# Two gate tiles per mLSTM head instead of three, thirds of a half tile, rows and gate in memory of their own

## The reference, cut to what matters

```
u = rmsnorm(x) * (1 + scale) + shift
aq, ak, av, az, mq, mk, mv, mo, mz, mg, ga, gb = split(u @ w_in)
y_b = attention(aq, ak, av) * silu(az)                      # 16 heads of 64
per mLSTM head of 256 (4 heads):
    h = forward scan + backward scan of (mq, mk, mv, gates) from the state C, n
    y_a = head_norm(h) * sigmoid(mo) * silu(mz)
merged = sigmoid(ga) * (y_a @ w_proj_a) + sigmoid(gb) * (y_b @ w_proj_b)
out = x + gate * rmsnorm(merged @ w_out)
```

## Time and profile before

| | us |
|---|---|
| median of 3 runs | 1960.53 (1960.12 to 1960.54) |
| profiled execution, its own time | 1960.23 |
| its span in the trace | 1958.4 |
| PE busy in the span | 1925.1 |
| DVE busy | 1204.3 |
| ACT busy | 667.2 |
| POOL busy | 109.8 |

### The profile page before, as it was taken

How to read it: one execution, slowest core, us unless ns; L and a number is a source line. 1 busy time by engine, 2 the same in 40 slices (tenths; PEclk the granted TensorE clock), 3 DMA queues, 4 the chain that set the end, 5 groups by cost and what they waited for, 6 DMA issues and landing times.

```text
span 1958.4 us, 31714 instructions
## 1 busy us (share of the span) xinstructions
PE 1925.1 (98%) x12298; PEld 1785.3 (91%) x12298; DVE 1204.3 (61%) x2065; ACT 667.2 (34%) x1015; POOL 109.8 (6%) x195
## 2 busy tenths in 40 slices
PE   6999999999999999999999999999999999999998
PEld 2589999999999999999898999889889999988886
DVE  3268766666666666665666664565556767783224
ACT  3443333333333333332555554233224222242221
POOL 2010000000000000000000000000002000000000
PEclk9999999999999999999999999999999999999999
DMA  9952353333333333334632323364454666634224
GB/s 372 398 181 77 114 166 112 112 112 112 112 112 112 112 112 112 112 112 114 196 98 82 123 83 118 91 150 134 109 130 143 196 208 184 209 114 140 81 75 161
DMA packets 297838, 273.95 MB, mean 140 GB/s; under 512 B 20016, under 2 KB 245048, under 8 KB 295840
## 3 DMA queue, kind: packets, MB, share of 16 engines
q1 hardware_dynamic: 283632, 216.71, 37.6%
q0 software_dynamic: 13824, 55.92, 7.9%
q10 hardware_dynamic: 304, 0.25, 0.0%
HBM read 235.01 MB, written 40.44 MB: 141 GB/s over the span
## 4 chain that ended last, share of the span: by engine, by line
PE 91%; DMA 3%; DVE 3%; SPq 1%; issue 1%; ACT 1%; POOL 0%; DVEq 0%; POOLq 0%; ACTq 0%
PE bank L2030 20%; PE bank L2110 12%; PE bank L2103 12%; PE bank L2104 12%; PE bank L2326 11%; PE bank L2039 10%; DMA WORK<-in_w_ada_dram 2%; PE bank L1949 2%; PE bank L2230 2%; PE bank L2005 2%; PE bank L2219 1%; PE bank L2171 1%; PE bank L2232 1%; PE bank L2148 1%; PE bank L1985 1%
## 5 line engine op out<-in xcount | busy, mean ns | idle before, releaser
L2030 PE MATMUL bank<-XH,WH 128*128 128x320 f32 x1472 | 345.5, 316 | 2.8 <-DVE XL L1823 2.1
L1026 ACT ACTIVATE WH<-RAW 128x1024 fp32r<-128x1024 f32 x195 | 206.6, 1060 | 386.3 <-PE bank L2110 306.3
L2030 PE MATMUL bank<-XL,WH 128*128 128x320 f32 x1472 | 335.2, 309 | 0.0
L1458 DVE TENSOR_TENSOR WL<-RAW,WH 128x1024 fp32r<-128x1024 f32 x195 | 238.4, 1222 | 142.3 <-ACT WH L1026 142.3
L905 ACT ACTIVATE WH<-RAW 128x1024 fp32r<-128x1024 f32 x122 | 129.1, 1059 | 530.5 <-PE bank L2039 406.1
L2030 PEld LDWEIGHTS bank<-XH,WH 128*128 128x128 f32 x1472 | 244.5, 188 | 10.8 <-issue 8.0
L2030 PEld LDWEIGHTS bank<-XL,WH 128*128 128x128 f32 x1472 | 246.2, 188 | 0.0
L2039 PE MATMUL bank<-XH,WL 128*128 128x320 f32 x1472 | 235.9, 310 | 0.0
L2039 PEld LDWEIGHTS bank<-XH,WL 128*128 128x128 f32 x1472 | 220.1, 188 | 4.1 <-issue 3.8
L2104 PE MATMUL bank<-XL,WH 128*128 128x320 f32 x720 | 212.5, 309 | 0.0
L2103 PE MATMUL bank<-XH,WH 128*128 128x320 f32 x720 | 212.4, 309 | 0.0
(11 more groups left out here) (241 smaller groups left out, 2968.8 us busy)
## 6 DMA issues: line engine op xcount, KB each, us to landing
RAW<-in_w_in_dram SPq DMA_DIRECT2D x165, 512.0 KB, 3.8
WORK<-in_w_ada_dram SPq DMA_DIRECT2D x71, 512.0 KB, 8.9
proj_dram<-OUTS POOLq DMA_DIRECT2D x92, 320.0 KB, 2.5
RAW<-in_w_out_dram SPq DMA_DIRECT2D x32, 512.0 KB, 3.7
RAW<-in_w_ada_dram SPq DMA_DIRECT2D x25, 512.0 KB, 9.2
WORK<-proj_dram SPq DMA_DIRECT2D x16, 640.0 KB, 4.6
WORK<-proj_dram POOLq DMA_DIRECT2D x32, 320.0 KB, 3.3
RAW<-in_w_proj_a_dram SPq DMA_DIRECT2D x16, 512.0 KB, 4.7
```

The costliest lines, as they stand in the source:

```text
L1026: ins = nc.scalar.activation(WH[:, (j + p) % 2, :], pair_raw(j, p), ACT.Copy)
L1458: V.tensor_tensor(WL[:, w, :], pair_raw(j, p), WH[:, w, :].bitcast(F32), ALU.subtract)\
L2030: pe.matmul(banks[n][:, 0:HALF_TOK], wh[:, k, :], x[:, k0 + k, n * HALF_TOK:(n + 1) * HALF_TOK], start=(first and k == 0 and wi == 0), sto ...
```

## The change

- `T_L1` goes from 64 to 68, `T_L2` from 78 to 82, `L2_TILES` from 3 to 2. Four gate tiles move from the plain tiles beside the mLSTM to two more pairs.
- A step goes with a third of a half tile: 16 products instead of 24. r = 1 to 12 now lie over two tiles.
- `HH` and the output gate (`MG`) get memory of their own. The row loads wait for `ml_qs` instead of `ml_ht`, the keys for `ml_sp` instead of `ml_zg`; the queries still wait for `ml_zg`. `states_out`, `state_loads` and the values of the next head follow each other.
- PE's backward state goes from r = 10 to 11, its transposes and DVE's gating from r = 11 to 12. On DVE the gate products stay at r = 10, the copy of the backward state (`ml_cbd`) goes to r = 11, in front of `lo`.
- The merge takes `w_proj_b` on the attention's blocks first. ACT makes their high parts before `ml_ya`, DVE five of their low parts at the last head's r = 11.
- POOL's power follows the gate loads in the same step, and a buffer for POOL's own DMA descriptors is set to 4096.

```diff
-T_PAIR, T_L1, T_L2, T_MERGE, T_OUT, T_END = 4, 64, 78, 90, 106, 122
+T_PAIR, T_L1, T_L2, T_MERGE, T_OUT, T_END = 4, 68, 82, 90, 106, 122
-L1_TILES, L2_TILES = 14, 3
+L1_TILES, L2_TILES = 14, 2
+LOW_EARLY = 5
+        HH = sb("HH", [P, 5, MD])
+        MG = sb("MG", [P, 2, TOK])
...
@@ SP
-                    sp.wait_ge(ml_zg, h)
+                    sp.wait_ge(ml_sp, h)
                 head_rows(h, MK, RB_MK, ml_kv)
...
-                    sp.wait_ge(ml_ht, h)
+                    sp.wait_ge(ml_qs, h)
                 for r in range(2):
                     sp.dma_start(RB[:, r, :], ...)
...
-                    if s == (3 if h == 0 else 6 * h + 3):
+                    if s == 4 * h + 3:
                         if h == 0:
                             head_values(0)
-                        head_keys(h)
-                        if h:
+                            head_keys(0)
+                        else:
+                            row_loads(h)
+                            head_keys(h)
                             head_queries(h)
-                    if s == 6 * h + 4:
+                    if s == 4 * h + 4:
                         if h == 0:
                             head_queries(0)
                             row_loads(0)
-                        if h:
+                        else:
                             states_out(h - 1)
-                    if s == 6 * h + 5:
-                        state_loads(h)
-                        if h + 1 < M_HEADS:
-                            head_values(h + 1)
+                            state_loads(h)
+                            if h + 1 < M_HEADS:
+                                head_values(h + 1)
@@ POOL
                     pool.wait_ge(ml_ub, 4 * h + 4)
-                    pool.wait_ge(ml_kw, h + 1)
-                    pool.dma_start(MK, head_rows(RB_MO, h)).then_inc(ml_gates_in, 16)
+                    pool.dma_start(MG[:, :, :], head_rows(RB_MO, h)).then_inc(ml_gates_in, 16)
                     pool.dma_start(MVT, head_rows(RB_MZ, h)).then_inc(ml_gates_in, 16)
-                if k == 2:
                     pool.wait_ge(ml_var, h + 1)
@@ ACT
-            act.wait_ge(ml_ya, M_HEADS + 1)
+            act.wait_ge(yb_done, 10 * KV_HEADS + 1)
             act.wait_ge(w_used, 2 * T_MERGE - 1)
-            high_y(range(8), y_hi)
+            high_y(range(8), y_hi, 8)
             evac(0, T_MERGE - 1)
             hi(0, 0, 2 * T_MERGE + 1)
+            act.wait_ge(ml_ya, M_HEADS + 1)
@@ DVE
+                    if r == 11:
+                        dve.wait_ge(ml_cb, h + 1)
+                        for cc in range(2):
+                            ins = V.tensor_copy(CA[:, 1, cc, :], ab[2 + cc][:, 0:257])
+                        ins.then_inc(ml_cbd, 1)
-                    if r == 11:
+                    if r == 12:
                         dve.wait_ge(ml_ht, h + 1)
...
-                if part and s + 1 < 2 * L2_TILES * M_HEADS:
+                if part == 1 and s + 1 < 2 * L2_TILES * M_HEADS:
                     lo(0, 0, 2 * T_L2 + s + 1)
+                if q == 6 * L2_TILES * M_HEADS - 2:
+                    low_y(range(LOW_EARLY), y_hi, y_lo, 8)
                 for h, r in phases(q):
                     if r == 10:
-                        dve.wait_ge(ml_cb, h + 1)
-                        for cc in range(2):
-                            ins = V.tensor_copy(CA[:, 1, cc, :], ab[2 + cc][:, 0:257])
-                        ins.then_inc(ml_cbd, 1)
                         z = MVT.rearrange("p c t -> p (c t)")
                         dve.wait_ge(ml_eg, h + 1)
...
+            low_y(range(LOW_EARLY, 8), y_hi, y_lo, 8)
             lo(0, 0, 2 * T_MERGE)
-            low_y(range(3, 8), y_hi, y_lo)
+            low_y(range(8, 12), y_hi, y_lo, 8)
             lo(0, 0, 2 * T_MERGE + 1)
-            low_y(range(8, KT), y_hi, y_lo)
+            low_y(range(12, KT), y_hi, y_lo, 8)
@@ PE
-                if r == 11:
+                if r == 12:
                     pe.wait_ge(ml_h, h + 1)
...
-                    if r == 10:
+                    if r == 11:
                         pe.wait_ge(ml_upd, h + 1)
                         state(1).then_inc(ml_cb, 1)
                 if part == 0:
...
-                    high_products(banks, w, 8 * x, range(0, 4), x == 0)
-                else:
-                    high_products(banks, w, 8 * x, range(6, 8), x == 0)
+                    high_products(banks, w, 8 * x, range(0, 3), x == 0)
+                elif part == 1:
+                    high_products(banks, w, 8 * x, range(4, 7), x == 0)
+                else:
                     pe.wait_ge(lo_done, 2 * t + x + 1)
-                    low_products(banks, w, 8 * x, x == 1, range(0, 4))
+                    low_products(banks, w, 8 * x, x == 1, range(0, 6))
                 for h, r in phases(q):
                     inside(h, r)
                 if part == 0:
-                    high_products(banks, w, 8 * x, range(4, 6), x == 0)
-                else:
-                    low_products(banks, w, 8 * x, x == 1, range(4, 8)).then_inc(w_used, 1)
-            pe.wait_ge(ml_ya, M_HEADS + 1)
+                    high_products(banks, w, 8 * x, range(3, 4), x == 0)
+                elif part == 1:
+                    high_products(banks, w, 8 * x, range(7, 8), x == 0)
+                else:
+                    low_products(banks, w, 8 * x, x == 1, range(6, 8)).then_inc(w_used, 1)
```

More of the change, by code:

```diff
@@ L674, in row_loads, with merge_half @@
                 if h:
-                    sp.wait_ge(ml_ht, h)
+                    sp.wait_ge(ml_qs, h)
                 for r in range(2):
                     sp.dma_start(RB[:, r, :], rrow[h + 4 * r, :].partition_broadcast(P)).then_inc(ml_in, 16)
[L679 to L682, removed]
+            def merge_half(i, k, x):
+                g = 2 * (T_MERGE + k) + x
+                w_half(4 * i + (g - 3), g, g % 4, (w_pb_v, w_pa_v)[x][:, :, bass.ds(P * k + 2 * P * i, P)])
+            for s in range(2 * L2_TILES * M_HEADS + 4):
+                if s < 2 * L2_TILES * M_HEADS:
+                    in_tile(T_L2 + s // 2, 0, COL_MERGE + P * (GATES_PAIRED + L1_TILES + s // 2), (s % 2,))
+                else:
+                    merge_half(0, (s - 16) // 2, s % 2)
                 for h in range(M_HEADS):
-                    if s == (3 if h == 0 else 6 * h + 3):
+                    if s == 4 * h + 3:
                         if h == 0:
                             head_values(0)
-                        head_keys(h)
-                        if h:
+                            head_keys(0)
+                        else:
+                            row_loads(h)
+                            head_keys(h)
                             head_queries(h)
-                    if s == 6 * h + 4:
+                    if s == 4 * h + 4:
                         if h == 0:
@@ L693, in _ @@
                             row_loads(0)
-                        if h:
+                        else:
                             states_out(h - 1)
-                    if s == 6 * h + 5:
-                        state_loads(h)
-                        if h + 1 < M_HEADS:
-                            head_values(h + 1)
+                            state_loads(h)
+                            if h + 1 < M_HEADS:
+                                head_values(h + 1)
+                    if s == 5 and h == 0:
+                        state_loads(0)
+                        head_values(1)
             def gada_load(i, m):
@@ L715, in out_piece @@
                 w_half(8 * n + (g - 3), g, g % 4, w_out_v[:, 2 * q:2 * q + 2, bass.ds(512 * n, 512)], k=2)
-            for k in range(2):
-                for x in range(2):
-                    merge_half(0, k, x)
             states_out(M_HEADS - 1)
@@ L862, in merge_gates @@
             def merge_gates(j, u):
-                for gi, rb in ((0, RB_GA), (1, RB_GB)):
+                for gi, rb in ((0, RB_GB), (1, RB_GA)):
                     pool.dma_start(GAB[:, u, gi, :], proj[bass.ds((rb + j) * P, P), :]).then_inc(sig_in[u], 16)
@@ L1161, in inter @@
                 nc.scalar.activation(ENM[:, :, :], COLH[:, :, 2:4], ACT.Exp).then_inc(ml_w, 1)
-            for q in range(4 * L2_TILES * M_HEADS):
-                s, part = divmod(q, 2)
+            for q in range(6 * L2_TILES * M_HEADS):
+                s, part = divmod(q, 3)
                 if part == 0:
@@ L1681, in _, with low_y @@
                         low_keys(kv, 3)
+            def low_y(ks, high, done, shift=0):
+                for k in ks:
+                    dve.wait_ge(high, k + 1)
+                    V.tensor_tensor(XL[:, k, :], Y[:, (k + shift) % KT, :], XH[:, k, :].bitcast(F32),
+                                    ALU.subtract).then_inc(done, 1)
             dve.wait_ge(m0_in, 16)
```

21 lines of the change are left out of this document (6 added, 15 removed).

## The result

The changed kernel takes 1975.67 us (median of 6 runs, 1972.78 to 1977.97); the kernel before took 1960.47 us beside it (1959.26 to 1960.66). The ratio is 1.0077, 95% interval 1.0067 to 1.0087: slower by 15.2 us. The forecast was 1967.4 us, range 1956 to 1974: the direction was right, the size was half of what came, and the median lies outside the range. The profiled execution took 1972.78 us, with a span of 1970.6 (before 1958.4, so +12.2).

A forecast was written before the change was run, and what follows sets the result against it. TensorE, never waiting in the mLSTM, was taken to bound the kernel. Terms -7.04 (products), +12.4 (hand-over), +1.2 (head 0) and +0.3 (merge's entry) sum to +6.9 us: forecast 1967.4 us, range 1956 to 1974.

The forecast's parts named there:

- 48 products, -7.04: Two pairs replace four plain tiles beside the mLSTM; PE saves 48 products, 7.04 us.
- The hand-over of `ab[2]`: r = 8 to 12 of each head: PE waits 3.1 us for DVE's copy of the backward state, +12.4 in all.
- Rival 1: The hand-over of `ab[2]` costs next to nothing, DVE's overhang being absorbed: 1955.0 us; chance 0.15.
- rival 3: The stall at the hand-over is halved: 1961.2 us, no change that shows; chance 0.09.
- Row of the head before, queries, scaled queries, gates hidden: mLSTM heads: `ml_ya`, next queries, read-out's scaled queries and gate loads come in time; no added wait of PE.
- Head 0, 1.2: First mLSTM head: rows and queries still wait for the attention, so PE waits for the transposed copies, +1.2 us.
- Merge's entry, +0.3: Start of the merge: PE waits for DVE's low parts, 3.7 us lost against 3.4 before, +0.3.
- State loads, taken as 0: Read-outs: loads behind the previous head's stores; one reading gave a 3.3 us stall in three heads, zero was taken.
- Rival 2: State loads come late, read-outs wait up to 3.3 us in heads 1 to 3: 1977.3 us; chance 0.10.
- The smaller buffer, taken as hidden: POOL's descriptor buffer at 4096 costs no instruction, and even DMAs that wait for one another would be hidden.
- The clock, taken as unaffected: TensorE's granted clock stays at 1.00 despite the new pauses in the mLSTM; nothing added.
- rival 4: Clock falls to 1.2 GHz after each 3.1 us pause, 4 x 3.7 = 15 us more: 1982; chance 0.02.

The follow-up runs named there:

- e9: e8 with nothing on DVE beside POOL's power, one `lo` in DVE's idle time, gate products behind the copy, forward state stored ahead of the queries: 1954.67 us.
- e1: The changed kernel with both gate products on DVE made over 8 of 1280 columns: 1960.32 us.
- e3: The kernel before, with only the copy of the backward state moved behind the gate products on DVE: 1975.99 us.
- e4: The kernel before with POOL's descriptor buffer at 4096 and nothing else: 1961.56 us.
- e2: The changed kernel with 20 overwritten filler products on PE between the fourth and fifth transpose of each head: 1970.81 us.
- e8: e7, with PE taking high by high, low weights, then low parts of `Y` for the merge's first tile: 1966.42 us.
- e5: The changed kernel with a head's state stores issued ahead of the step's weight half on SP: 1973.14 us.
- e10: e9 with the norm weight's load issued on ACT's queue instead of POOL's: 1955.40 us.
- e6: The changed kernel with DVE reordered: first gate product during POOL's power, normalising, backward copy, second product, `lo` behind the gating: 1967.39 us.
- e7: e6 with state stores first, a semaphore of their own for queries, and head 0's transposed copies ahead of its decay arguments: 1968.27 us.

## Why the prediction went wrong

By its own steps:

- **48 products, -7.04:** right. 32 pairs at 24.68 us. The span of e9, which waits almost nowhere, is 1951.2, 7.2 under before: -7.0 for the products, -1.0 for shorter waits at the merge's entry, +0.8 for the four small waits elsewhere.
- **The hand-over of `ab[2]`, 3.1 us per head:** right, 2.97 measured. That DVE's order makes it was shown from both sides: e1 without the two products' time, e3 with the order alone on the kernel before. Rival 1 (absorbed) and rival 3 (halved) are out.
- **Row of the head before, queries, scaled queries, gates hidden:** right; no wait of PE at any of them in heads 1 to 3.
- **Head 0, 1.2:** 1.40 measured.
- **Merge's entry, +0.3:** about right in price, though after doesn't show it: of the 2 us that I named before the sixth block 0.31 came, since the low clock ahead of it had slowed PE. Without that, in e1, the two waits are 1.71 and 0.29, together 2.0 as before (2.05).
- **State loads, taken as 0:** mis-sized. Rival 2's mechanism was there, 1.26 and 0.57 us. First store to first load took 15.8 us in head 1 and not the 9 that I read off the last head; the row with the store between two heads was the nearer one. The bound of 3.3 held in every experiment (2.87 at most).
- **The smaller buffer, taken as hidden:** a miss of 1.36 us in the profile of after, 0.87 of PE's time in the trace of e4. I looked at POOL in the mLSTM only; the DMA that it delays stands 230 us later, and behind it DVE.
- **The clock, taken as unaffected: the step that failed.** The sum with what was measured in all other terms is 1967.4 - 0.5 (waits 11.86, not 12.4) + 0.2 + 1.8 + 1.4 - 0.4 (merge, -0.1 for +0.3) = 1969.9, inside the range. In the profiled execution the clock adds 1.8 net, and with the 1.1 that isn't listed that is its 1972.8, still inside. The median is 2.9 higher. e2, which takes only the four pauses' low clock away, gains 4.9 us of median (about 1 to 7 by the intervals). By that the clock is the largest of the three terms that I had put at nothing; that it makes up all of the 2.9 us is not shown. I gave rival 4 a chance of 0.02 on one row: a stretch at the start of the program whose 4.6 us of idle time came in many pieces, beside work of another kind. A pause of 3 us in the mLSTM is not that, and the row was one draw: in the traces of e1, e2 and e8 the clock does fall for 3.4 to 6.8 us in this opening, between 22 and 30 us. The Trainium skill, TensorE: Matmul & The Clock Gate, Part 1: The HAM clock gate, was the better guide to the direction; the traces agree in part: of after's four pauses of 2.95 to 2.97 us two were followed by a low stretch, of e3's four all. My price in the rival was too high in the other way, 3.7 us for each pause instead of 1.2 to 1.6 for each low stretch.

What stays open: which pauses are followed by a low stretch. The traces hold 2.87, 2.24 and 2.03 us (yes), 2.17 and 2.10 us (no), 1.72 and 1.69 (yes), 1.71 (no, twice). Since several of these lie so close together, the length of one pause doesn't decide it alone. None came behind the waits of 0.9 to 1.5 us in the mLSTM and at the merge's entry. But in e5 one began at 1762.5 us, in the output projection, behind waits of 1.13 and 0.40 us, and in e10 one came at the merge's entry among waits of 0.18 us. I didn't try to separate it from what PE does around the pause.

That the low clock comes of the waits and isn't a thing of the new kernel's other work: e3 has it on the old kernel, e1 loses it on the new one and e2 loses it at the transposes, and e9, with no wait over 0.2 us there, has none in the mLSTM or the merge's entry.

## What to carry to other kernels

Where TensorE has been busy without a break, a new wait costs its length and, for 14 of the 21 here of 1.7 to 3.0 us, some 1.2 to 1.6 us more for the lower clock at its end, less where a further wait stands right behind it; a forecast has to carry both. When an engine's work is moved, put what releases the bottleneck engine first and what merely fills last: the same work in another order, on VectorE above all, but for the state's stores and the merge's first products too, was worth 21 us of 1976 here. A wait that goes uncovers the next one, and a new order can make one: in e6 the waits for the state loads grew from 1.8 to 5.8 us, and only with all waits treated did the 7 us of products saved show in the time.

## What the runs showed of the hardware

- **VectorE and GpSimd in each other's way.** GpSimd's power on 128x5 takes 1.20 us, and 2.35 to 2.37 us in all four heads of e6 while VectorE multiplies two operands of 128x1280 in memory for 1.48 us. The gain of filling that gap was eaten by it. The Trainium skill, SBUF — State Buffer, section Who interferes with whom, says that a VectorE instruction with two inputs in SBUF contends with a GpSimd instruction that reads SBUF; the traces agree.
- **The stores of a head's state.** Eight stores, four of them of one four-byte element per partition, took 9 to 13 us from the last issue to the load that waits for their landing (12.7 in e7 and 12.1 in after in head 1, 9.1 in e6), though all of them together are 0.5 MB. That the four-byte ones hold it up is not shown: in after they land 9.5 us after their issue in the median, and the others, of 128 KB, 8.8. In e9, where half of them go out 8 us ahead of the others, it is still 11.7 us from the last issue; the load came 5.1 us earlier mostly because that last issue did, by 4.1.
- **A low stretch at a pause** lasts 3.4 us in nearly all cases; in e5 one was twice as long, at the first of its waits. Kernels with many pauses also scatter more: e8's 12 runs reach over 10 us, e9's 6 over 2.5. How much of that is the clock was not measured.
